# A decoder layer on one Trainium2 core: GpSimd adds the residual behind the mix norm instead of VectorE

## The reference

```python
hn = rmsnorm(x, w_pre_mix)
z = hn @ w_in
...
mix = jnp.concatenate([o_g, o_s.astype(x.dtype)], axis=-1) @ w_out
h = x + rmsnorm(mix, w_post_mix)
f = rmsnorm(h, w_pre_ffn)
f = (jax.nn.silu(f @ w_gate) * (f @ w_up)) @ w_down
h = h + rmsnorm(f, w_post_ffn)
h = h + jax.nn.sigmoid(h @ w_ple_gate) * (p @ w_ple_proj)
```

## Time and profile before

| | |
|---|---|
| time before, median of 3 runs | 2829.82 us (2828.7 to 2829.92) |
| the profiled execution: its time, its span | 2830.93 us, 2828.8 us |
| TensorE busy | 2714.7 us, 96% of the span |
| weight loads busy | 2263.8 us, 80% |
| VectorE busy | 1209.9 us, 43% |
| ScalarE busy | 851.0 us, 30% |
| GpSimd busy | 238.5 us, 8% |

### The profile page before, as it was taken

One profiled execution on the slowest core, in us unless ns is written; L12 is line 12 of the kernel. 1 busy time (PEld: TensorE's weight loads), 2 busy tenths in 40 slices (PEclk: granted clock), 3 DMA queues, 4 the chain that ended last, 5 costly groups with the idle time before them and its releaser, 6 DMA issues.

```text
span 2828.8 us, 38154 instructions
## 1 busy us (share of the span) xinstructions
PE 2714.7 (96%) x15072; PEld 2263.8 (80%) x15072; DVE 1209.9 (43%) x2110; ACT 851.0 (30%) x1680; POOL 238.5 (8%) x416
## 2 busy tenths in 40 slices
PE   6999999999999979999999999999999989999987
PEld 4777777877777759978777777877777979999987
DVE  5455552555555473134433556344234461111143
ACT  4344532443334343122222243332222331000021
POOL 0033000111100000111110002121210000000000
PEclk9999999999999999999999999999999999999998
DMA  7865577777776676745544576444445665444453
GB/s 252 299 205 181 202 289 238 263 253 249 243 246 237 252 283 199 235 159 181 180 153 175 201 247 204 161 161 160 150 155 182 233 216 188 164 164 164 164 183 123
DMA packets 215777, 579.40 MB, mean 205 GB/s; under 512 B 28320, under 2 KB 66080, under 8 KB 215200
## 3 DMA queue, kind: packets, MB, share of 16 engines
q1 hardware_dynamic: 214960, 574.87, 58.7%
q0 software_dynamic: 640, 2.10, 0.2%
HBM read 430.41 MB, written 147.65 MB: 204 GB/s over the span
## 4 chain that ended last, share of the span: by engine, by line
PE 85%; DVE 7%; DMA 3%; ACT 2%; issue 2%; SPq 1%; POOL 0%; DVEq 0%; ACTq 0%; POOLq 0%
PE ps L1862 75%; PE ps L1935 2%; DMA wld<-wl 1%; PE ps L1955 1%; PE ps L2013 1%; PE ps L2048 1%; DVE wl L1467 1%; DVE bl L1562 1%; PE ps L2032 1%; DVE ssq L1519 1%; PE ps L2037 1%; DMA wl<-wld 1%; PE ps L1871 1%; PE ps L2002 1%; DVE mixF L1543 1%
## 5 line engine op out<-in xcount | busy, mean ns | idle before, releaser
L1862 PE MATMUL ps<-bh,wh 128*128 128x512 f32 (+1 forms) x2352 | 774.3, 363 | 9.6 <-DVE bl L1562 5.3
L1862 PE MATMUL ps<-bl,wh 128*128 128x512 f32 (+1 forms) x2352 | 757.9, 356 | 0.0
L1862 PE MATMUL ps<-bh,wl 128*128 128x512 f32 (+1 forms) x2352 | 757.8, 356 | 0.0
L1862 PEld LDWEIGHTS ps<-bh,wh 128*128 128x128 f32 x2352 | 418.0, 189 | 84.6 <-issue 12.0
L1862 PEld LDWEIGHTS ps<-bh,wl 128*128 128x128 f32 x2352 | 418.3, 189 | 63.1
L1862 PEld LDWEIGHTS ps<-bl,wh 128*128 128x128 f32 x2352 | 418.6, 189 | 58.6 <-issue 1.7
L1862 PE MATMUL ps<-gh,wh 128*128 128x512 f32 (+1 forms) x880 | 291.9, 364 | 15.7 <-DVE mixF L1491 8.6
L1862 PE MATMUL ps<-gl,wh 128*128 128x512 f32 (+1 forms) x880 | 285.6, 357 | 0.0
L1862 PE MATMUL ps<-gh,wl 128*128 128x512 f32 (+1 forms) x880 | 285.3, 357 | 0.0
L1862 PE MATMUL ps<-dh,wh 128*128 128x512 f32 (+1 forms) x768 | 263.9, 374 | 17.5 <-DVE dl L1562 9.6
L1862 PE MATMUL ps<-dl,wh 128*128 128x512 f32 (+1 forms) x768 | 255.1, 363 | 0.0
(11 more groups left out here) (191 smaller groups left out, 2860.1 us busy)
## 6 DMA issues: line engine op xcount, KB each, us to landing
wh<-whd SPq DMA_DIRECT2D x306, 512.0 KB, 3.6
wl<-wld SPq DMA_DIRECT2D x306, 512.0 KB, 4.5
w_raw<-in_w SPq DMA_DIRECT2D x102, 512.0 KB, 4.6
whd<-wh SPq DMA_DIRECT2D x102, 512.0 KB, 5.5
wld<-wl SPq DMA_DIRECT2D x102, 512.0 KB, 6.2
zt<-zd SPq DMA_DIRECT2D x16, 1024.0 KB, 7.8
zd<-zst SPq DMA_DIRECT2D x56, 256.0 KB, 5.0
res_m<-in_x SPq DMA_DIRECT2D x24, 256.0 KB, 6.1
```

The lines of the kernel that those rows point to most:

```text
L1862: last = MM(out, ww[SLOT[n]][:, w_], xx[:, kk, r_], start=(j == 0 and x == 0), stop=(j == len(ks) - 1 and x == 2))
```

## The change

In the norms M0 to M3 VectorE no longer adds the residual; for P0 to P3 it still does. GpSimd gets a new step for the same parts: it waits for the residual's load and for VectorE's multiplication of that tile, and adds in place. It raises the same semaphore, so those who wait for the sum are unchanged.

```diff
+            def add_residual(name, ks):
+                for k in ks:
+                    src = norm_src(name, k)
+                    gp.wait_ge(r_in[k], 16 * (ADDS.index(name) + 1))
+                    gp.wait_ge(v_nm, NORMS.index(name) * KM + k + 1)
+                    TT(src, src, residual(name, k), ALU.add).then_inc(v_res, 1)
+
...
                         if s[0] == "tile":
                             tile(*s[1:])
+                        elif s[0] == "nm" and s[1][0] == "M":
+                            add_residual(*s[1:])
...
-                if kind in "MP":
+                if kind == "P":
                     for k in ks:
                         src = norm_src(name, k)
                         dve.wait_ge(r_in[k], 16 * (ADDS.index(name) + 1))
```

## The result

The changed kernel takes 2839.44 us (median of 8 runs, 2835.59 to 2844.18), the kernel before 2829.28 us in the same comparison (8 runs, 2827.06 to 2835.18). The ratio is 1.0037, with a 95% interval from 1.0028 to 1.0047: 10.2 us longer, slower by more than the measurement is uncertain. The forecast was 2840 us.

What follows compares the result with a forecast made beforehand. TensorE, busy 96% of the span, was taken as the bound, waiting at M1 to M3 for VectorE's sums. 2830.93 + 10.5 = 2841.4 us profiled; the run median lies 1.1 lower, so 2840 us, range 2828 to 2848.

Steps and rivals of the forecast that it cites:

- Where the change can act: At M1, M2 and M3, TensorE's `mean` waits for VectorE's sums of squares, 25.4 us in all; not at M0.
- What it takes from VectorE, 14.9 us: Eight adds fewer at each of M1, M2, M3: 4.8, 4.8 and 5.3 us less, if nothing else happened.
- The price of a pair, 1.68 us: At M1 and M2, one VectorE instruction and one GpSimd add take turns: 0.55 + 1.13 us; M3 scaled to 1.89.
- the sign: At M2, an add recorded with 1.6 to 1.8 us, the VectorE instruction beside it with 1.2 to 1.7 us.
- third term, 6.2: M3's share, in us, of the 17 us upper bound on the lengthening, if nothing overlaps even at the hand-over.
- The sum, 10.5 us: Total lengthening from taking turns: 3.3 us at M1, 3.3 at M2 and 3.9 at M3.
- about 13, 10 and 12.5 us: Forecast waits of `mean` for VectorE's sums at M1, M2 and M3 in the changed kernel.
- What is hidden: M0's eight adds end near 416.3, before F0's first square at 418.64, so M0 costs nothing; cover 2.3 us.
- The rival of late weights: SyncE's stores delay weight loads until TensorE waits, adding some us at each place; inside the forecast's upper part, no separate chance.
- The clock: TensorE's clock around the three waits: 0 in the sum, 5 us allowed in either direction in all.
- The adds lie beside VectorE's queue: At M1 to M3, GpSimd's adds do not hold VectorE up and the waits shrink: 2815 us, chance 0.12.
- Some adds fall into holes: At M1 to M3, some adds run free while VectorE waits for squares: about 2830 us, chance 0.14.

Runs made afterwards that it cites:

- experiment 7: Against the kernel before: GpSimd adds the residual at M0 alone, VectorE still adds at M1, M2 and M3; 2829.4 us, ratio 0.9998.
- experiment 1: Against the changed kernel: GpSimd adds only the first column of each residual tile, same waits and signals, result not the layer's; 2813.05 us.
- experiment 5: Against the changed kernel: root, gate tiles and partial sums of squares beside M1 to M3 put in PSUM, GpSimd still adding; 2815.47 us.
- experiment 2: Against the kernel before: VectorE adds as before, GpSimd makes as many extra adds on tiles nobody waits for; 2848.02 us, ratio 1.0065.
- experiment 3: Against the kernel before: GpSimd fills tiles nobody waits for with zeros, only writing, at the places of the adds; 2828.39 us, ratio 0.9998.
- experiment 4: Against the changed kernel: only the root of the M norms put in PSUM, where the multiplications read it; 2831.0 us, ratio 1.0006.
- experiment 6: Against the kernel before: VectorE still adds the residual, with root, gate tiles and partial sums of squares in PSUM; 2830.15 us, ratio 1.0000.

## Why the prediction held, step by step

**Where the change can act.** Right: M0 does nothing to the time (experiment 7), and the difference lies at M1, M2 and M3.

**What it takes from VectorE, 14.9 us.** Right as the gain if nothing else happened: experiments 1 and 5 gained 16.5 and 14.1 us against the kernel before.

**The price of a pair, 1.68 us.** The groups by form of the changed kernel give it over all 32 adds; count, busy us and mean ns:

```profile
L1077 POOL TENSOR_TENSOR mixO<-mixO,res_m 128x512 f32<-128x512 f32 x24 | 40.1, 1698 | 427.2 <-DVE mixO L1552 427.2
...
L1077 POOL TENSOR_TENSOR mixO<-mixO,res_m 128x576 f32<-128x576 f32 x8 | 14.9, 1886 | 186.8 <-DVE mixO L1552 186.8
```

An add took 1.70 us with 512 columns and 1.89 with 576, where 1.68 had been taken from the earlier trace rows and 1.89 scaled from it. One meeting of two instructions, in a part of the kernel far from the change, was enough to price 32. That it fits to 1% is in part luck: the dead adds of experiment 2, of the same operation and width, took 1.49 us, and beside an add `tb` took 1.78 us, a little more than the 1.2 to 1.7 us that were named as the sign.

Experiments 2 and 3 show turns beside a GpSimd instruction that reads SBUF (two of VectorE's adds in 2.98 us; 2848.02 us in all) and none beside one that only writes (1.29 us; 2828.39 us). Experiments 4 and 5 show none for a VectorE instruction that takes one of its two tensors from PSUM (four multiplications in 2.72 us beside GpSimd's adds, 4.81 with both tensors in SBUF; 2831.0 and 2815.47 us). From above the prediction had bounded the sum by 17 us, with a pair of 1.96 us; its third term, 6.2, comes to 6.4. The stretches show 10.4 us.

**The sum, 10.5 us.** Measured 10.4 us over the three stretches and 10.2 us between the medians. The prediction's waits "about 13, 10 and 12.5 us" came out as 12.2, 10.2 and 12.5. M1's is smaller because 0.8 us of that stretch went to another wait: TensorE waits 3.2 us for `wl` instead of 2.4, as the prediction had said of it ("about 1 us longer").

**What is hidden.** At M0 the eight adds end at 415.76, forecast 416.3, and the first square follows at 418.27, when its eviction allows. In the changed kernel's timeline:

```profile
402.66 13.10 POOL L1077 TENSOR_TENSOR mixO<-mixO,res_m 128x512 f32<-128x512 f32 x8 [106.66 <-DVE mixO L1552]
...
417.78 0.60 ACT L1122 ACTIVATE zst<-ps 128x512 f32<-128x512 f32 x1 [5.02 <-PE ps L1871]
418.27 0.62 ACT L1188 ACTIVATE ssq<-mixO 128x512 f32<-128x512 f32 x1
```

SyncE's weight load behind M2:

```profile
1703.17 0.37 SPq L755 DMA_DIRECT2D wh<-whd  x1
```

It left at 1703.17 rather than at 1696.86. Of these 6.3 us M2's first multiplication was already 2.2 us later; the other 4.1 us are the "some 4 us" of the prediction. No new wait for weights appeared in TensorE's waits (5.9 us for `wl` from DRAM in the whole span, before 6.0). The rival of late weights is out.

**The clock.** It was left at 0 with 5 us to either side, from the 0.79 of the 8 us behind M2. Windows of the changed kernel at M2; us, then PE, PEld, DVE, ACT and POOL busy, PE clock, DMA:

```profile
1706.00:1708.00 2.00, 1.69 (x3) 0.84 (x3) 1.55 (x3) 1.17 (x1) 0.00 (x0) 0.50 0.88 332
1708.00:1710.00 2.00, 2.00 (x7) 1.49 (x6) 0.19 (x1) 1.32 (x2) 0.00 (x0) 0.69 1.03 410
1710.00:1712.00 2.00, 2.00 (x10) 1.59 (x10) 1.93 (x3) 0.00 (x0) 0.00 (x0) 1.00 0.98 388
```

and of the kernel before:

```profile
1704.00:1706.00 2.00, 2.00 (x6) 1.59 (x5) 1.65 (x3) 0.24 (x1) 0.00 (x0) 0.50 0.93 373
1706.00:1708.00 2.00, 2.00 (x9) 1.58 (x8) 0.48 (x1) 0.00 (x0) 0.00 (x0) 0.90 0.01 4
```

In both kernels the granted clock stood at 0.50 when `mean` began. After the change it was 1.00 from 1710 on, 1.6 us into the unit behind `mean` (1708.38); before, it was 0.50 until 1706, 3.1 us into that unit (1702.86). That returned 1.2 us, by the two durations of that unit, in one execution each. It can't be put down to the longer wait: in experiments 3, 6 and 7, where M2's wait is 6.9 us as in the kernel before, the same unit took 7.49, 6.39 and 6.11 us, and in experiment 2, with a wait of 13.7 us, 7.11. What sets it is open; the term's 0 stands, and its 5 us of room covered these differences.

**The rivals.** "The adds lie beside VectorE's queue" named 2815 us as its price. It is wrong for this kernel, and experiment 5 lies there to half a microsecond: what decided between them was which operands lie in SBUF, and not which engine was idle. "Some adds fall into holes" found no holes.

## What to carry to other kernels

An engine that the profile shows as idle need not be free to take work: look first at what the busy engine's instructions read during that time. Here VectorE's elementwise instructions on two SBUF tensors and GpSimd's adds from SBUF took turns (`tb` took 1.78 us beside an add and 0.69 without), and a first price, 1.68 us a pair, stood in the trace where two such instructions already met; take it from there, and allow for another operand pattern (1.49 against 1.70 us). If the work is to move all the same, put one operand of VectorE's instructions in PSUM where banks are free; here that turned 10 us of loss into 14 us of gain.

## What was not expected of the hardware

A PSUM operand cost VectorE nothing that shows: `ps<-ps,pjb` 0.69 us against 0.69 for `tb<-ta,pjb`, and 2.30 us for three sums against 2.28. The expectations of experiments 5 and 6 count with some 0.06 us for each read of PSUM; no run shows it. In the trace of before `ssq<-ps,cols,ssq` takes 0.75 us and `rs<-ssq,rs` 0.69, but `mixO<-mixO,cols,rs`, without PSUM, takes 0.75 on average too, and experiment 6 took 2830.15 us (ratio 1.0000) where 2 to 4 us more were expected. And in experiment 2 the price of a dead add to VectorE was 0.85 us, not the 1.13 us that the earlier trace rows show for GpSimd's part of one turn, nor the 1.0 us of an add of the change.
